# An output projection as seven products of quarters instead of one plain product, in a one-core encoder block

## The reference

```python
merged = jax.nn.sigmoid(gate_m) * (y_m @ w_branch_m[l]) + jax.nn.sigmoid(gate_h) * (y_h @ w_branch_h[l])
x = x + merged @ w_out[l]

u = rmsnorm(x, norm_x_g[l])
mn = rmsnorm(mem, norm_mem_g[l])
q_x = (u @ w_q_x[l]).reshape(bsz, seq, X_HEADS, X_HEAD_DIM)
```

## Time and profile before

| | |
|---|---|
| time, median of 3 runs | 2569.84 us (2569.46 to 2571.01) |
| the profiled execution: time, span | 2574.76 us, 2573.0 us |
| granted TensorE clock, mean | 0.997 of full speed |
| PE / DVE / ACT / POOL busy | 99% / 64% / 36% / 29% |

### The profile page before, as it was taken

One profiled execution on the slowest core, in us unless ns is written; L12 is line 12 of the kernel. 1 busy time (PEld: TensorE's weight loads), 2 busy tenths in 40 slices (PEclk: granted clock), 3 DMA queues, 4 the chain that ended last, 5 costly groups with the idle time before them and its releaser, 6 DMA issues. The chain is left out here.

```text
span 2573.0 us, 35010 instructions
## 1 busy us (share of the span) xinstructions
PE 2538.4 (99%) x13888; PEld 2199.1 (85%) x13888; DVE 1644.8 (64%) x1839; ACT 915.2 (36%) x1123; POOL 752.6 (29%) x705
## 2 busy tenths in 40 slices
...
GB/s 284 117 79 128 102 104 125 139 125 89 98 99 107 107 93 112 107 156 156 145 142 157 170 123 213 34 194 184 155 34 147 70 128 115 103 110 178 282 195 180
DMA packets 184195, 346.49 MB, mean 135 GB/s; under 512 B 10236, under 2 KB 113992, under 8 KB 184033
## 3 DMA queue, kind: packets, MB, share of 16 engines
...
## 5 line engine op out<-in xcount | busy, mean ns | idle before, releaser
L2273 PE MATMUL ps<-whi,a_hi 128*128 128x256 f32 x1024 | 294.9, 288 | 1.4 <-DVE a_lo L2027 1.1
L2273 PE MATMUL ps<-whi,a_lo 128*128 128x256 f32 x1024 | 289.6, 283 | 0.0
L2273 PE MATMUL ps<-wlo,a_hi 128*128 128x256 f32 x1024 | 289.6, 283 | 0.0
L2242 PE MATMUL ps<-a_hi,whi 128*128 128x512 f32 x608 | 248.1, 408 | 0.2 <-DVE a_lo L1589 0.2
L2242 PE MATMUL ps<-a_hi,wlo 128*128 128x512 f32 x608 | 237.3, 390 | 0.0
L2242 PE MATMUL ps<-a_lo,whi 128*128 128x512 f32 x608 | 236.9, 390 | 0.0
L1570 DVE TENSOR_TENSOR wlo<-raw,whi 128x2048 fp32r<-128x2048 f32 x61 | 142.0, 2329 | 132.4 <-ACT whi L946 132.1
L2273 PEld LDWEIGHTS ps<-whi,a_hi 128*128 128x128 f32 x1024 | 196.2, 192 | 2.2 <-DVE a_lo L2027 1.3
L2273 PEld LDWEIGHTS ps<-wlo,a_hi 128*128 128x128 f32 x1024 | 196.4, 192 | 0.3 <-issue 0.2
L2273 PEld LDWEIGHTS ps<-whi,a_lo 128*128 128x128 f32 x1024 | 196.2, 192 | 0.0
L946 ACT ACTIVATE whi<-raw 128x2048 fp32r<-128x2048 f32 x61 | 117.0, 1917 | 191.8 <-PE ps L2273 111.1
...
## 6 DMA issues: line engine op xcount, KB each, us to landing
raw<-in_w_in SPq DMA_DIRECT2D x45, 1024.0 KB, 6.5
raw<-in_w_up SPq DMA_DIRECT2D x22, 1024.0 KB, 5.0
hg_T<-ev ACTq DMA_DIRECT2D x32, 512.0 KB, 2.9
qfb<-hg_T POOLq DMA_DIRECT2D x24, 512.0 KB, 6.7
...
down_weight_sums<-wd POOLq DMA_DIRECT2D x22, 512.0 KB, 4.4
hidden_T<-ga ACTq DMA_DIRECT2D x11, 1024.0 KB, 4.0
hidden_sums<-s POOLq DMA_DIRECT2D x10, 1024.0 KB, 4.7
```

What stands on the lines that cost most here:

```text
L2242: ins = pe.matmul(ps[:, u], W[sw][:, b.slot, k, c * P:(c + 1) * P], op[mw][:, k, t * HALF:(t + 1) * HALF], start=k == 0 and q == 0, stop=k ...
L2273: ins = pe.matmul(ps[:, u, part * BC:(part + 1) * BC], op[sw][:, k, t * P:(t + 1) * P], W[mw][:, b.slot, k], start=k == 0 and q == 0, stop ...
```

## The change

The out stage becomes seven products of quarters (512 tokens x 512 of the width x 512 columns). With A the merged activations (a11 is tokens 0 to 511, k tiles 0 to 3) and B the weights, sums s1 to s4 of quarters of A and t1 to t4 of quarters of B are made first: those of A on DVE (`out_sum`), those of B on POOL (`out_weight_sum`). Product i takes 4 token tiles x 4 k x 3 matmuls of 512 columns, so the stage has 336 of them. The results are not combined with each other in PSUM but added into quarters of the residual `acc`: the residual is loaded in quarters, the last one into a spare buffer `o2`, and three sums of residual quarters (one on DVE, two on POOL) spread what one product gives to several quarters. In the order of the products, their operands are: a11 b11; a12 b21; s2 t2; s3 t3; s1 t1; a12's sum s4 with b22; a22 with t4. `w_out` is loaded as four quarters, the last two (b12, b22) into `out_b12` and `out_b22`, which lie over buffers of the branch stage: b12 after the last matmul of that stage, b22 after `split_lo(Blk(B_OUT + 1))`. `kx`, `vx` and the gain `gb_A` are loaded behind the POOL sums; the first block of `w_q_x` behind the second of them and `split_lo(Blk(B_OUT + 2))`.

```diff
-            for b0, name in ((B_OUT, "w_out"), (B_Q, "w_q_x"), (B_O, "w_o_x")):
+            w_o = wk("w_out")
+            for j in range(4):
+                b = Blk(B_OUT + j)
+                sp.wait_ge(w_lo, b.count(-2))
+                if j == 2:
+                    sp.wait_ge(unit_done, Blk(B_BRANCH + 7).unit(3))
+                elif j == 3:
+                    sp.wait_ge(br_done, 16)
+                sp.dma_start(wide(raw, b) if j < 2 else out_w[j - 2],
+                             w_o[:, 4 * (j % 2):4 * (j % 2) + 4, at(j // 2 * HALF, HALF)]).then_inc(w_ld[b.slot], 16)
+            sp.wait_ge(s_t, OUT_T + 2)
...
                 for j in range(4):
                     if b0 == B_O and j == 2:
                         sp.wait_ge(unit_done, Blk(B_Q + 3).unit(3))
@@ -578,7 +621,7 @@
 
                 i, g = divmod(p, NFF)
                 if p >= RING:
-                    sp.wait_ge(prod_done, PART0 + p - RING + 1)
+                    sp.wait_ge(prod_done, PROD0 + p - RING + 1)
                 else:
                     sp.wait_ge(unit_done, product(N_WIN - 1, 2 if p < 4 else PRODUCTS - 1))
                 l, r = LEFT[i], RIGHT[i]
@@ -869,13 +912,42 @@
             pool.wait_ge(unit_done, Blk(B_BRANCH + 6).unit(3))
             operand_loads(a_raw, mergedT, range(KT - 2), a_ld)
             pool.wait_ge(unit_done, Blk(B_BRANCH + 7).unit(3))
-            for j in range(4):
-                pool.dma_start(acc[:, :, j * BC:(j + 1) * BC], x[:, j * BC:(j + 1) * BC].rearrange("(t p) n -> p t n", p=P)) \
-                    .then_inc(x_ld[j], 16)
+            def x_quarter(j, dst, r, h):
+
+                pool.dma_start(dst, x[at(r * HALF, HALF), at(h * HALF, HALF)].rearrange("(t p) n -> p t n", p=P)).then_inc(x_ld[j], 16)
+
+            for r, h in ((0, 0), (0, 1), (1, 0)):
+                x_quarter(2 * r + h, acc[:, 4 * r:4 * r + 4, at(h * HALF, HALF)], r, h)
+
+            def out_weight_sum(i, dst, x_, y_):
+
+                signal(pool, pool.tensor_tensor(dst, x_, y_, ALU.subtract), s_t, OUT_T + i + 1)
+
+            b11, b21 = wide(raw, Blk(B_OUT)), wide(raw, Blk(B_OUT + 1))
+            b12, b22 = out_w[0], out_w[1]
+            pool.wait_ge(w_lo, Blk(B_OUT).count())
+            pool.wait_ge(w_ld[Blk(B_OUT).slot], Blk(B_OUT + 2).slot_dmas())
+            out_weight_sum(0, b11, b12, b11)
             pool.wait_ge(br_done, 16)
+            pool.wait_ge(w_ld[Blk(B_OUT + 1).slot], Blk(B_OUT + 3).slot_dmas())
+            out_weight_sum(1, ev[:], b22, b11)
+            out_weight_sum(2, b12, b22, b12)
+            pool.wait_ge(w_lo, Blk(B_OUT + 1).count())
+            out_weight_sum(3, b21, b21, ev[:])
+            pool.wait_ge(s_sum, 8)
+            pool.wait_ge(op_lo, 2 * KT + 4)
+            x_quarter(3, o2[:], 1, 1)
+            pool.wait_ge(s_ev, OUT_TAKEN + 8)
+            u3 = acc[:, 4:8, HALF:D]
+            for i, (dst, y_) in enumerate(((acc[:, 4:8, 0:HALF], u3), (u3, o2[:]))):
+                pool.wait_ge(x_ld[2 + i], 16)
+                signal(pool, pool.tensor_tensor(dst, dst, y_, ALU.add), s_t, OUT_T + 5 + i)
+            pool.wait_ge(*out_done(4, 3))
+            pool.dma_start(kx[:], kxT_d.rearrange("(k p) m -> p k m", p=P)).then_inc(keys_ld, 16)
+            pool.wait_ge(part_lo, PART0 + 2)
+            pool.dma_start(vx[:], vx_d.rearrange("(c p) n -> p c n", p=P)).then_inc(keys_ld, 16)
+            pool.wait_ge(part_lo, PART0 + 3)
...
+            def out_weight_hi(n, dst, src):
+
+                signal(act, act.activation(dst, src, ACT.Copy), part_hi, PART0 + n + 1)
+
+            for t in range(4):
+                act.wait_ge(*out_done(0, t))
+                signal(act, act.activation(acc[:, 4 + t, HALF:D], ps[:, t], ACT.Copy), ev_done, Blk(B_OUT).unit(t))
+            act.wait_ge(s_sum, 6)
+            quarter_hi(3, o2[:], quarter(a_hi, 0, 0))
+            act.wait_ge(s_t, OUT_T + 2)
+            out_weight_hi(0, wide(whi, Blk(B_OUT)), ev[:])
+            quarter_hi(4, quarter(a_sum, 0, 1), o3_hi[:])
+            act.wait_ge(s_sum, 7)
+            quarter_hi(5, quarter(a_raw, 0, 1), o1_hi[:])
+            quarter_hi(6, quarter(a_raw, 1, 1), quarter(a_hi, 1, 1))
+            act.wait_ge(s_t, OUT_T + 3)
+            act.wait_ge(*out_done(1, 3))
+            out_weight_hi(1, wide(whi, Blk(B_OUT + 1)), out_w[0])
+            act.wait_ge(s_sum, 8)
+            quarter_hi(7, quarter(a_sum, 0, 1), quarter(a_hi, 1, 0))
+            act.wait_ge(*out_done(2, 3))
+            split_hi(Blk(B_OUT + 2))
+            act.wait_ge(*out_done(3, 3))
+            out_weight_hi(2, wide(whi, Blk(B_OUT + 1)), out_w[1])
+            act.wait_ge(s_t, OUT_T + 4)
+            act.wait_ge(*out_done(4, 3))
+            act.wait_ge(op_lo, 3 * KT)
+            signal(act, act.activation(quarter(a_hi, 0, 1), wide(raw, Blk(B_OUT + 1)), ACT.Copy), w_hi, Blk(B_OUT + 3).count())
+            split_hi(Blk(B_Q))
...
-            natural_add(B_OUT, 0)
+            def out_weight_lo(n, src, hi, lo):
+
+                dve.wait_ge(part_hi, PART0 + n + 1)
+                signal(dve, dve.tensor_tensor(lo, src, hi, ALU.subtract), part_lo, PART0 + n + 1)
+
+            def out_add(i, *tiles):
+
+                r, h = {0: (0, 0), 1: (0, 0), 2: (1, 1), 3: (1, 1), 4: (1, 1), 5: (0, 1), 6: (1, 0)}[i]
+                for t in tiles:
+                    dve.wait_ge(*out_done(i, t))
+                    if i == 0:
+                        dve.wait_ge(ev_done, Blk(B_OUT).unit(t))
+                    a = acc[:, 4 * r + t, at(h * HALF, HALF)]
+                    signal(dve, dve.tensor_tensor(a, a, ps[:, out_bank(i) + t], ALU.add), *out_taken(i, t))
+                    if i in (2, 5, 6):
+                        dve.sem_inc(ev_done, 1)
+
+            s1_, s3_ = quarter(a_raw, 0, 1), quarter(a_sum, 0, 1)
+            a22, acc12 = quarter(a_raw, 1, 1), acc[:, 0:4, HALF:D]
+            slot0, slot1 = Blk(B_OUT), Blk(B_OUT + 1)
+            out_sum(6, o2[:], a22, s3_, ALU.subtract)
+            out_sum(7, s1_, s1_, a22, ALU.add)
+            dve.wait_ge(x_ld[0], 16)
+            out_add(0, 0, 1, 2, 3)
+            quarter_lo(3, o2[:], quarter(a_hi, 0, 0), quarter(a_lo, 0, 0))
+            out_weight_lo(0, ev[:], wide(whi, slot0), wide(wlo, slot0))
+            quarter_lo(4, s3_, o3_hi[:], o3_lo[:])
+            out_add(1, 0, 1, 2, 3)
+            out_weight_lo(1, out_w[0], wide(whi, slot1), wide(wlo, slot1))
+            line(dve.tensor_tensor(s3_, quarter(a_hi, 1, 0), o2[:], ALU.subtract))
+            out_sum(8, s3_, s3_, quarter(a_lo, 1, 0), ALU.add)
+            out_add(2, 0, 1, 2, 3)
+            dve.wait_ge(x_ld[1], 16)
+            line(dve.tensor_tensor(acc12, acc12, acc[:, 4:8, HALF:D], ALU.add))
+            quarter_lo(5, s1_, o1_hi[:], quarter(a_lo, 0, 1))
+            split_lo(Blk(B_OUT + 2))
+            out_add(3, 0, 1, 2, 3)
+            quarter_lo(6, a22, quarter(a_hi, 1, 1), quarter(a_lo, 1, 1))
+            quarter_lo(7, s3_, quarter(a_hi, 1, 0), quarter(a_lo, 1, 0))
+            out_weight_lo(2, out_w[1], wide(whi, slot1), wide(wlo, slot1))
+            for t in range(4):
+                dve.wait_ge(*out_done(4, t))
+                line(dve.tensor_tensor(acc12[:, t], acc12[:, t], ps[:, t], ALU.add))
+            dve.wait_ge(s_t, OUT_T + 6)
+            out_add(4, 0, 1, 2, 3)
+            dve.wait_ge(w_hi, Blk(B_OUT + 3).count())
+            signal(dve, dve.tensor_tensor(quarter(a_lo, 0, 1), wide(raw, slot1), quarter(a_hi, 0, 1), ALU.subtract), w_lo, Blk(B_OUT + 3).count())
+            split_lo(Blk(B_Q))
+            out_add(5, 0, 1, 2)
+            norm_mul(10, na)
+            out_add(5, 3)
+            norm_mul(11, na)
+            norm_mul(12, na)
+            for t in range(NT):
+                if t < 4:
+                    out_add(6, t)
+                norm_lo(10 + t, t, a_hi, a_lo)
+                if t + 3 < NT:
+                    norm_mul(10 + t + 3, na)
...
-            natural(B_OUT, 2 * KT, 10, (range(KT - 2), range(KT - 2, KT)))
+            def out_pe(i, left, right):
+
+                for t in range(4):
+                    if i == 0:
+                        wait_bank(Blk(B_OUT), t)
+                    elif i >= 2:
+                        pe.wait_ge(*out_taken(i - 2, t))
+                    for k in range(4):
+                        for q, (sw, mw) in enumerate(((0, 0), (0, 1), (1, 0))):
+                            ins = pe.matmul(ps[:, out_bank(i) + t], left[sw][:, k, t * P:(t + 1) * P], right[mw][:, k],
+                                            start=k == 0 and q == 0, stop=k == 3 and q == 2)
+                    if t == 3 and i in OUT_SLOT:
+                        ins.then_inc(unit_done, 4)
+                    else:
+                        ins.then_inc(prod_done, 1)
+                    if i == PRODUCTS - 1:
+                        norm_tr(10 + t, na)
+
+            a11, a21, a12, a22 = [[quarter(t, k, h) for t in opA] for k in range(2) for h in range(2)]
```

(68 more changed lines are left out.)

53 lines of the change are left out of this document (31 added, 22 removed).

## The result

The changed kernel takes 2578.03 us (median of 8 runs, 2576.5 to 2585.0), the kernel before 2569.83 beside it (8 runs): ratio 1.0032, 95% interval 1.0023 to 1.0041, or 8.2 us more. The forecast was 2576.8.

The account below looks back on a forecast made before the run. PE was 99% busy, but DVE's list, held off by POOL, would end the changed out stage: Q starts 7.9 us later, less 0.9 for late tiles, net +7.0 on 2569.84, so 2576.8 us; range 2574.5 to 2579 (0.56).

Parts of the forecast that it names:

- What PE saves: Out stage: 768 matmuls at 0.120 us become 336 at 0.2267, 92.2 to 76.2 us, 16.0 less on PE.
- DVE's list: DVE's out-stage work up to `n_lo` 14 sums to 82.2 us, ending 2.1 us behind PE, plus 23.2 held off by POOL.
- POOL's operation: Each of six 128x2048 sums on POOL takes 4.63 us, extrapolated from rows of 512 and 1024 elements.
- The waits: DVE operations reading SBUF wait for POOL's: five at 4.35 us and one of 1.4, together 23.2.
- Where they meet: POOL's sums placed against particular DVE operations; PE then waits 13 us before product 2 and 7.6 before product 5.
- Q's first groups: Start of Q: its first four groups lost 0.9 us to late tiles before; these now come in time, -0.9.
- The profiled execution: Whole kernel: the profiled run's 4.9 us above the median is the profiler's and stays; 2574.76 becomes 2581.8.
- Transfers: Loads in the out stage cost nothing: same bytes for `w_out` and `x`, gain covered by 2.5 us, `w_q_x` by some 30.
- A: Rival: POOL's long operations don't hold DVE up in the out stage, so the gain comes through; 2553.6 us, chance 0.10.
- B: Rival: three more POOL operations fall beside DVE's PSUM sums, saving 8.7 us of waits; 2568.1 us, chance 0.22.
- C: Rival: transfers are late too, b22 costing 3 us and the gain 1.5; 2581 us and above, chance 0.12.

Follow-up runs that it names:

- 8: Changed kernel with 32 instead of 48 matmuls in each of the seven products, 112 fewer in all: 2579.9 us, ratio 1.0040 to the kernel before.
- 1: Changed kernel with all six POOL sums cut to 32 of 512 columns, every wait kept: 2558.2 us, ratio 0.9942 to the kernel before.
- 2: Changed kernel with only the four weight sums on POOL cut to 32 of 512 columns: 2566.3 us, ratio 0.9982 to the kernel before.
- 6: Changed kernel with products 2 and 3 added onto product 0's PSUM banks, 5 onto 4's, and POOL's residual sums dropped: 2571.3 us, ratio 1.0000 to before.

## Why the prediction was right, step by step

- **What PE saves, 16.0 us.** The matmuls are 336 at 0.227 where the clock is at its upper level, as forecast (the 216 ns of the Trainium skill, "TensorE: Matmul & The Clock Gate", section "Back-to-back issue gap", weighed there, do not fit them; the section gives them for an isolated matmul, and 131 for a stream, which fits less). But the term was never in the result: 8 takes 25 us more from PE and gains nothing. PE's saving only decided how much of it became waits. So it was also wrong to say that by 216 ns the result would be 4.6 us later: in the prediction's own sum DVE stands 2.1 + 23.2 us behind PE, and a smaller saving would have shortened waits.
- **DVE's list, 82.2 us and 23.2 of being held off.** From the low part of three k tiles at 1561.84 to the end of `n_lo` 14, which started at 1667.03 and took 1.23, it is 106.4 us, against 105.4 forecast. It began 0.8 us before the stage's first matmul, where I had it 0.1 behind. So Q came at +8.0 instead of +7.9.
- **POOL's operation, 4.63 us.** 4.61 alone, in the row at 1578.92. The line through the rows of 512 and 1024 elements held for four times the size.
- **The waits, 5 x 4.35 + 1.4.** They were 4.29, 1.77, 4.21, 4.24, 4.29, 4.23: 23.0 in all. The five long ones are some 0.1 shorter than I had, the short one 0.4 longer. The Trainium skill ("SBUF — State Buffer", section "SBUF: two separate sides") has the whole of POOL's operation as the wait; these rows show 4.2 to 4.3 of 4.61, so the lock is confirmed, with 0.3 to 0.4 us less than the whole, of which I had taken off 0.28 for two hand-overs.
- **Where they meet.** This was partly wrong. I had t1 hold up `s2`; it came earlier and held the low part of 512 elements ahead of `s2`. I had t2 behind `s2` and `s1` held up. b22 landed later (t2 began 16.3 us into the stage, forecast 14.7), so `s1` kept its 2.29 and t2 met the PSUM sums; t3 then held `wlo<-ev` of product 2, where I had t4, and t4 `o_lo` of product 3. PE's wait before product 2 was 6.9 us and not 13, one of 2.7 came before product 4, and 5.6 instead of 7.6 before product 5. The sum stayed, since it is a count of meetings; that the count came out the same, five long and one short, with t2 and t3 in each other's place, is luck.
- **Q's first groups, -0.9.** This is the term that failed: it was +1.1. The late tiles did come in time: Q's second and third groups took 7.3 us with their transposes, against 7.8 before. But the first took 4.4 against 2.9. Behind its wait of 2.26 us Q's matmuls start 0.43 us apart. Rows of PE, and the windows of the same places (the figure before the last two is the granted clock):

```profile
1668.90 0.63 PE L2419 MATMUL ps<-a_lo,whi 128*128 128x512 f32 x1
1669.33 0.63 PE L2419 MATMUL ps<-a_hi,wlo 128*128 128x512 f32 x1
1669.76 0.63 PE L2419 MATMUL ps<-a_hi,whi 128*128 128x512 f32 x1
```

```profile
1591.50:1594.50 3.00, 2.23 (x5) 1.82 (x6) 2.97 (x2) 1.81 (x1) 3.00 (x1) 0.50 0.00 0
1597.00:1600.00 3.00, 3.00 (x15) 2.46 (x14) 2.93 (x3) 0.00 (x0) 0.00 (x0) 1.00 0.02 5
1637.50:1640.00 2.50, 2.50 (x6) 2.02 (x7) 2.40 (x4) 0.00 (x0) 0.58 (x1) 0.50 0.85 297
1668.50:1671.50 3.00, 3.00 (x8) 2.32 (x9) 2.93 (x3) 0.71 (x2) 0.82 (x2) 0.50 0.02 5
```

  0.50 is the lower of the two levels, 1.2 GHz. Before the change Q waited 0.17 us and ran at 1.00. I had counted a wait as its length alone. After all, 2576.8 lay 1.2 us under the median, and this term is 2.0 of the 2.1 us by which the two stages together, +9.1, missed the +7.0.
- **The profiled execution, 4.9 us above the median.** I had called this difference the profiler's and the same after. It was 0.2 after: 2578.25 against 2578.03. The profiled span grew by 3.5 us and the median by 8.2, with +9.1 in the two stages, so the rest of this trace was 5.6 us shorter in code that is the same. Had I forecast the profiled execution (2581.8), I would have been some 3.5 us too high; the error of 1.2 us of the median, where the sum missed the stages by 2.1, is in part luck.
- **Transfers, nothing.** Right for the changed kernel: no wait of PE or DVE in the stage ends with a load. 1, 2 and 6 show that it was near.
- **The rivals.** A (2553.6) needed POOL not to hold DVE; with POOL cut short the time is 2558.2, so its price was about right (the 2.7 us of waits for ScalarE are part of the difference) and its condition did not hold. B: one meeting of six fell beside PSUM sums, as forecast, not four. C: b22 was 1.6 us later than forecast, but cost only the order of meetings.
